# Hybrid attention: ScalarE copies the older unit's transposes ahead of the new unit's exponential or sigmoid

## What is computed

```python
# kind 0, 4 heads with two score matrices each
p = softmax(where(allowed, q @ k.T * scale, -inf)); w = p[0] - lam * p[1]; o = w @ v
# kind 1, 8 heads, stick breaking: sigmoids and a running product
a = where(strict, exp(log_sigmoid(z) + log_rest), 0);  o = a @ v
# kind 2, 8 heads, with a forgetting bias
p = softmax(q @ k.T * scale + cum_log_f[q] - cum_log_f[k]);  o = p @ v
```

## Time and profile before

| | us |
|---|---|
| median of 3 runs | 3238.56 (3236.24 to 3239.3) |
| the profiled execution | 3236.32 |
| its span from first to last instruction | 3234.5 |
| attention of layer 0 in the profile | 320.25 to 450.31 |
| attention of layer 1 | 864.86 to 998.36 |

### The profile page before, as it was taken

One profiled execution on the slowest core, in us unless ns is written; L12 is line 12 of the kernel. 1 busy time (PEld: TensorE's weight loads), 2 busy tenths in 40 slices (PEclk: granted clock), 3 DMA queues, 4 the chain that ended last, 5 costly groups with the idle time before them and its releaser, 6 DMA issues.

```text
span 3234.5 us, 36328 instructions
## 1 busy us (share of the span) xinstructions
PE 3049.3 (94%) x14559; PEld 1675.0 (52%) x14559; DVE 1526.7 (47%) x2852; ACT 726.6 (22%) x1521; POOL 330.1 (10%) x195
## 2 busy tenths in 40 slices
PE   8999899998989899999998999999999888899998
PEld 5888443787744344456755533333335544444443
DVE  5993942998482434765565222222243762111112
ACT  1211532121262211121124100000014652111111
POOL 4553000655200000000001000000000000000000
PEclk9999999999999899999999999999999999999999
DMA  5442003455201222010412798888841003999997
GB/s 221 169 183 96 10 1 125 158 192 225 79 1 39 106 81 107 33 52 30 161 65 93 331 376 338 351 343 331 348 176 52 27 3 138 379 421 421 421 421 294
DMA packets 87625, 598.23 MB, mean 185 GB/s; under 512 B 10456, under 2 KB 11259, under 8 KB 16932
## 3 DMA queue, kind: packets, MB, share of 16 engines
q1 hardware_dynamic: 79776, 575.70, 44.5%
q10 hardware_dynamic: 5524, 12.35, 1.1%
q0 software_dynamic: 2160, 7.87, 0.6%
HBM read 590.64 MB, written 5.24 MB: 184 GB/s over the span
## 4 chain that ended last, share of the span: by engine, by line
PE 63%; DVE 7%; ACT 2%; issue 1%; another core or an unknown queue 0%; DVEq 0%; ACTq 0%; PEldq 0%
PE ps L1358 8%; PE ps L2727 7%; PE ps L2689 7%; PE ps L2706 3%; PE ps L2770 3%; PE ps L2740 3%; PE ps L2601 3%; PE ps L1091 3%; PE ps L3013 2%; PE ps L2584 2%; PE ps L2779 2%; PE ps L2500 2%; PE ps L1456 2%; PE ps L1696 2%; PE ps L3174 1%; PE ps L1508 1%
## 5 line engine op out<-in xcount | busy, mean ns | idle before, releaser
L610 PE MATMUL ps<-mem 128*128 128x256 f32 x1792 | 393.3, 381 | 12.7 <-DVE mem L640 10.8
L610 PEld LDWEIGHTS ps<-mem 128*128 128x128 f32 x1792 | 340.2, 191 | 65.2 <-DVE mem L640 14.7
L555 POOL TENSOR_TENSOR mem<-mem 128x512 f32<-128x512 f32 (+1 forms) x160 | 302.0, 1887 | 544.4 <-DVE mem L851 284.8
L2868 DVE TENSOR_TENSOR mem<-ps,mem 128x512 f32<-128x512 f32 x32 | 22.1, 692 | 547.0 <-PE ps L2689 313.4
L753 DVE SCALAR_TENSOR_TENSOR mem<-mem 128x1024 f32<-128x1024 f32 x160 | 255.3, 1635 | 13.4 <-DMA mem<-in_ada_w 13.4
L1358 PE MATMUL ps<-mem 128*128 128x512 f32 (+1 forms) x768 | 253.5, 492 | 2.9 <-ACT mem L1199 2.9
L2727 PE MATMUL ps<-mem 128*64 128x512 f32 x1024 | 223.3, 594 | 0.0
L2689 PE MATMUL ps<-mem 128*64 128x512 f32 x1024 | 222.5, 592 | 0.7 <-ACT mem L2626 0.7
L1358 PEld LDWEIGHTS ps<-mem 128*128 128x128 f32 x768 | 147.1, 193 | 108.6 <-issue 97.2
L640 DVE TENSOR_TENSOR mem<-ps,mem 128x256 f32<-128x256 f32 x308 | 121.2, 418 | 111.8 <-PE ps L610 68.3
L1091 PE MATMUL ps<-mem 128*128 128x512 f32 x384 | 169.6, 597 | 1.8 <-DVEq L156 1.8
(11 more groups left out here) (412 smaller groups left out, 4071.5 us busy)
## 6 DMA issues: line engine op xcount, KB each, us to landing
mem<-in_moe_w SPq DMA_DIRECT2D x384, 1024.0 KB, 14.0
mem<-in_w_in SPq DMA_DIRECT2D x48, 1024.0 KB, 8.3
mem<-in_ada_w SPq DMA_DIRECT2D x48, 1024.0 KB, 4.9
mem<-in_hy_w_in SPq DMA_DIRECT2D x24, 1024.0 KB, 7.0
mem<-in_w_out SPq DMA_DIRECT2D x12, 1024.0 KB, 6.9
mem<-in_k_win_l SPq DMA_DIRECT2D x8, 1024.0 KB, 6.9
mem<-in_hy_w_out SPq DMA_DIRECT2D x8, 1024.0 KB, 4.9
mem<-in_sw_w_in SPq DMA_DIRECT2D x6, 1024.0 KB, 7.2
```

The lines of the kernel that those rows point to most:

```text
L555: gp(out, x, y, op).then_inc(A.mark(sem), 1)
L610: m = mm(seven(l, unit), x[:, k, :], y[:, k, :], start=(k == 0), stop=(k == 3))
```

## The change

In `act_attn` the block that copies the transposes of unit s-3 is moved, as it is, ahead of the block that takes the exponentials or the sigmoid of unit s. No instruction and no wait is added or removed, and the streams of TensorE and VectorE stay the same, row by row.

```diff
         def act_attn(A):
             mxn = 0
             for s in range(len(UN) + LAG):
+                if s >= LAG:
+                    u = s - LAG
...
+                    A.e.wait_ge(S["turned"], u + 1)
+                    if i == 0 and hh >= 2:
+                        A.e.wait_ge(S["o_full"], hh if hh == 4 else hh - 1)
...
+                    act(dst, src, ACT.Copy).then_inc(A.mark("turned_out"), 1)
                 if s < len(UN):
...
-                if s >= LAG:
-                    u = s - LAG
...
-                    act(dst, src, ACT.Copy).then_inc(A.mark("turned_out"), 1)
             end_phase(A)
```

More of the change, by code:

```diff
@@ L988, in act_attn @@
             for s in range(len(UN) + LAG):
+                if s >= LAG:
+                    u = s - LAG
+                    kind, pair, i = UN[u]
+                    hh = u // NQ
+                    A.e.wait_ge(S["turned"], u + 1)
+                    if i == 0 and hh >= 2:
+                        A.e.wait_ge(S["o_full"], hh if hh == 4 else hh - 1)
+                    n, b = (1, 4 + u % 2) if kind == 0 else (2, 4)
+                    dst = weights_t(hh).rearrange("p c (j q) -> p c j q", q=512)[:, :, 0:i + 1, i * P:(i + 1) * P]
+                    src = ps[:, b:b + n, 0:(i + 1) * P].rearrange("p c (j q) -> p c j q", q=P)
+                    act(dst, src, ACT.Copy).then_inc(A.mark("turned_out"), 1)
                 if s < len(UN):
```

## The result

The changed kernel takes 3217.56 us (median of 4 runs, 3213.8 to 3218.3) where the kernel before takes 3238.93 (median of 4, 3236.24 to 3241.47). The ratio is 0.9932, with a 95% interval of 0.9915 to 0.9949. That is 21.4 us less; the forecast had 17.6. The profiled execution is the one of 3216.99 us, with a span of 3215.2.

What follows compares the result with a forecast made beforehand. TensorE's matmuls are busy 94% of the span; VectorE bounds kind 1, TensorE kind 2, no engine is full over layer 0's phase. 2.6 + 1.0 - 0.4 + 1.8 + 3.8 = 8.8 us a layer, 17.6 in all: 3221.0 us, range 3215 to 3230.

Steps and rivals of the forecast that it cites:

- rival 2: Inside both attention phases: with the waits gone, half-clock stretches may go too, 2.8 us more, 3218.2 us; chance 0.13.
- Kind 0, and kind 0 to kind 1: Heads 1 to 4 and the passage to the sigmoid heads: VectorE's waits shrink, 2.6 and 1.0 us a layer gained.
- Kind 1: Heads 5 to 8, bound by VectorE: no gain; unit 19's sigmoid, behind a copy awaiting PV, costs 0.4 us a layer.
- The cover inside kind 1: Heads 5 to 8: the sigmoid behind a copy still ends before VectorE's scan, with 0.45 us to spare.
- Kind 1 to kind 2: Passage from head 8 to 9: copy ahead of the table load lets unit 35's scores start 1.8 us sooner.
- Kind 2: Heads 9 to 12, bound by TensorE: its waits for copies go, 1.27 us a head, 3.8 us a layer.
- The fit that the forecast hung on: Kind 2: copies ready for the transposes with 0.16 us to spare, exponentials for the scores with 0.35.
- Rival 1: Kind 2: scores wait for exponentials instead, so its 3.8 us go in both layers, 3228.6 us; chance 0.13.
- Rival 3: Waits put down to the copy really end with something else, so nothing moves, 3238.6 us; chance 0.05.
- Rival 4: Kinds 0 and 2: exponentials held behind transposes and copy cost 19 us a layer, 3276 us; chance 0.04.

Runs made afterwards that it cites:

- e1: Kernel before with copies put first only in the steps of kind 0 (heads 1 to 4): 3230.83 us, ratio 0.9969.
- e4: Kernel before with copies put first in kinds 0 and 2, kind 1 left in its old order: 3216.78 us, ratio 0.9926.
- e7: Kernel before, old order, with each copy of kind 2 (heads 9 to 12) issued twice: 3260.3 us, ratio 1.0066.
- e6: Changed kernel, new order, with each copy of kind 2 (heads 9 to 12) issued twice: 3234.81 us, ratio 0.999 to the kernel before.
- e2: Kernel before with copies put first only in the steps of kind 2 (heads 9 to 12): 3224.4 us, ratio 0.9945.
- e5: Changed kernel with step 19 put back, unit 16's copy behind unit 19's sigmoid: 3215.33 us, ratio 0.9931 to the kernel before.
- e3: Kernel before with copies put first only in the steps of kind 1 (heads 5 to 8): 3243.39 us, ratio 1.0018.

## Why the prediction was right, and where it was off

**The whole.** Three profiles each of before and after give both phases in 265.8 and 243.7 us: 22.1 less. The rest of the kernel took 2971.3 and 2971.0 us on the mean, so all of the gain lies in the phases; over all 14 profiles the rest, which no edit touches, lies between 2967.5 and 2975.1 us, and differences of a few us between medians are no finer than that. Worked out from distances: from PV 1 to PV 12 the order gives 110.56 - 102.32 = 8.24 us a layer. The way to the first PV shrank by 0.57 on the mean (16.85 to 16.28). Stretches at 1.2 GHz behind it added 2.24 us a layer before and none after. 8.24 + 0.57 + 2.24 = 11.05, twice is 22.1. The forecast of 3221.0 was 3.4 us too high; rival 2's 3218.2 is nearest to the 3217.56 measured. The forecast left out rival 2's part, and that was the larger of its two errors: 2 x 2.24 = 4.5 us, less the 0.9 by which the first PV fell short of the 1.0 a layer, against 0.8 by the order.

**Kind 0, and kind 0 to kind 1: right, at 3.6 us a layer.** The prediction had 2.6 + 1.0. By PV starts e1 and e4 show 2.6 between PV 1 and PV 4 and about 1.0 ahead of the first PV, with heads of 8.06 and 8.63 where 8.7 was said. That looks like another split, but a PV's start also moves by the PV's own wait, 0.72 to 1.08 us for the first in before and its repeats. On VectorE, by which the prediction argued, the split holds. The waits of 1.29 us at 340.48 and 350.48 are 0.32 and nothing in layer 0 of after, and nothing in its layer 1. From the maxima of unit 8 to those of unit 12 it is 10.00 before and 8.63 after (1.37), from there to the first scan of kind 1 11.77 before, 10.61 in e1 (1.16) and 10.88 after. From unit 4 to unit 8 it is 9.79 in e7 and 8.75 in e6 (1.04).

How much the first PV gains goes with the granted clock ahead of it. From the phase's first scores to the first PV, mean us:

| granted clock there | old order in kind 0 | new order in kind 0 |
|---|---|---|
| 0.78 to 0.80 | 16.76 (5 layers) | 15.66 (9) |
| 0.68 to 0.70 | 16.97 (4) | 16.08 (2) |
| 0.60 to 0.61 | 17.55 (3) | 17.36 (5) |

So the 1.0 is there at the two higher levels, and only 0.2 at the lowest, where the first PV has no wait in the old order either (e2). Two of the six layers of after and its repeats were at the lowest, none of before, which is why the mean gain is 0.57.

**Kind 1: -0.63 instead of -0.4.** The wait behind the sigmoid of unit 19 is there and costs 0.36 (e5), where 0.4 was said. The 0.27 at the start of kind 1 stood in the term before it, as part of the 0.5 by which the copy of unit 13 puts off the table load. The cover inside kind 1 holds: heads of 9.83.

**Kind 1 to kind 2: 1.72, where 1.8 was said.** The scores of unit 35 now wait for the exponentials, as the prediction had it. Layer 0 of the kernel after:

```profile
400.81 1.13 PE L947 MATMUL ps<-mem 64*128 64x512 f32 x4 [0.52 <-ACT mem L1015]
...
402.63 1.23 DVE L1039 TENSOR_REDUCE mem<-ps 128x2 f32<-128x1024 f32 x1 [0.21 <-PE ps L952]
```

VectorE waits 0.21 us of the 1.93 in the earlier trace rows.

**Kind 2: the term that was mis-sized.** A head gained 1.51 us, not 1.27, so 4.5 a layer for 3.8. The mechanism was right and the list of waits too short. On the timeline of before, besides the two waits of the earlier trace rows, the eight transposes between them also wait:

```profile
424.77 0.81 ACT L1016 ACTIVATE mem<-ps 128x768 f32<-128x768 f32 x1
425.63 0.86 PEld L965 LDWEIGHTS ps<-mem 128*128 128x128 f32 x8
425.63 1.09 PE L965 MATMUL ps<-mem 128*128 128x128 f32 x8
```

They start 0.05 us behind the copy's end, and 0.11 later than they could; no bracket marks it, since a gap this small isn't put down to a releaser. That makes 1.38. The other 0.13 is in the transposes themselves. Before, those that waited have weight load and matmul begin together, as here at 425.63. After, the load runs ahead:

```profile
407.17 0.64 PEld L965 LDWEIGHTS ps<-mem 128*128 128x128 f32 x6
407.23 0.82 PE L965 MATMUL ps<-mem 128*128 128x128 f32 x6
```

From the transposes to the next scores it is 0.80, 1.02 and 0.36 us for six, eight and two of them before, and 0.75, 0.97 and 0.32 after.

The fit that the forecast hung on held: no scores of kind 2 wait for exponentials, and the transposes begin at 407.23, 0.28 us behind the end of the copy (0.60 us from 406.35), with nothing to wait for.

**The sum by order** is then 3.6 - 0.6 + 1.7 + 4.5 = 9.2 us a layer, 18.4 in all, where 17.6 was said. That is with the first PV's gain of 1.0.

**The clock.** The remaining 3 us fit rival 2, a direction that the prediction had seen and given 0.13. In the phases it is some 3.6: 4.5 given back behind the first PV, 0.9 lost ahead of it. Its price for one stretch, 1.4 us, is of the right size: those counted above added 0.6 to 2.6 each. Its number was too low. It took one a layer from the one row that it had; the six layers of the old order in full have 8 of them, at 1.7 us on the mean. And the 0.96 over layer 0 that it took as a sign of them was none. Busy time by stretch, split at the first PV, shows where the clock is low (third from the end; of 1.0). Layer 0 of before, at full clock behind the first PV:

```profile
320.25:337.38 17.13, 13.07 (x60) 5.68 (x60) 12.68 (x36) 10.06 (x33) 0.00 (x0) 0.70 0.28 115
337.38:450.31 112.93, 95.70 (x621) 52.89 (x621) 86.80 (x172) 66.63 (x162) 0.00 (x0) 1.00 0.00 1
```

Layer 0 of after, then layer 1 of before:

```profile
319.02:336.40 17.38, 14.37 (x60) 6.47 (x61) 11.97 (x35) 10.18 (x33) 0.00 (x0) 0.61 0.28 111
336.40:441.98 105.58, 93.06 (x624) 52.18 (x622) 88.28 (x173) 65.59 (x163) 0.00 (x0) 1.00 0.00 1
```

```profile
864.86:881.50 16.64, 11.66 (x59) 5.22 (x59) 12.58 (x36) 10.06 (x33) 0.00 (x0) 0.79 0.29 119
881.50:998.36 116.86, 98.76 (x621) 54.00 (x621) 87.49 (x173) 66.64 (x162) 0.00 (x0) 0.97 0.00 1
```

Behind the first PV after is at full clock throughout. Ahead of it both are far below, by a varying amount, and the way there takes 15.4 to 17.4 us in kernels with the new order in kind 0. So a part was given back there: in the first pair of profiles the phase of layer 0 reaches its first PV 0.25 us later than before, not 1.0 sooner.

**Rivals 1, 3 and 4.** Rival 1 is out: heads of kind 2 have no wait of TensorE left. Rival 3 is out by e1 and e2. Rival 4's mechanism exists in two places, the sigmoid of unit 19 and the start of kind 1; together they are 0.63 us a layer in the change and 0.94 alone (e3), where 19 was its price.

**What stays open.** Why a wait of 1.68 us brings the clock down at one PV and not at the same PV of the other layer. It may not be chance alone: of the 12 layers with the old order in kind 0, the second PV was slow in the three that reached the first in 16.65 us and in the three that did in 17.54 or 17.55, and in none of the six in between (16.68 to 17.13). That pattern was seen afterwards and is not tested. That the waits themselves bring the clock down, and not something else in the order, fits all counts, e6 and e7 above all, but no run sets one such wait by itself. And the medians don't tell after, e4 and e5 apart; that kind 1 is better left in the old order is shown by the distances and by e3, not by the time of e4.

## What to carry to other kernels

When an engine takes its queue in order and serves two stages of a staggered pipeline, put ahead the work whose input is there first and whose result the fullest engine wants first; it is the order of arrival that counts, not the age of the unit. Look at each seam between kinds of work by itself: the same move gained 1.5 us a head in one regime, nothing in another, and lost 0.36 us where the copy waited for a long PV just issued. And count what a wait does to the clock with what it takes itself.

## What the hardware showed that was not expected

- The drain of kind 2 has the same three waits of 0.69, 0.90 and 1.11 us in before and after. The last PV behind them ran at half clock in 4 of 6 profiled layers of before (and of its repeats), in none of the 4 layers of e1 and e3, and in 1 of 14 of the kernels in which kind 2 has the new order. Layer 1 of before, and of after:

```profile
993.47 4.01 PE L982 MATMUL ps<-mem 128*64 128x512 f32 x16 [1.11 <-ACT mem L1016]
```

```profile
975.74 2.38 PE L982 MATMUL ps<-mem 128*64 128x512 f32 x16 [1.11 <-ACT mem L999]
```

  What differs is the work ahead of the drain: 1.4 us lost to waits in each head before, none after. That gaps in the heads ahead cost a later place its clock fits these counts but isn't shown: e1 and e3 have the same gaps in kind 2 and never lost it there.
- Groups of two to eight transposes take 0.04 to 0.05 us less to the next matmul where they didn't wait, and a PV of kind 0 0.10 less (2.42 in the earlier trace rows, 2.32 after). In the rows above the weight load starts 0.06 us ahead of the matmul there, and with it behind a wait. A wait costs a little more here than its length.
